# Constant 16-bit matmuls placed in TensorE's waits inside each norm of a ten-stage transformer kernel

## What is computed

```python
def rmsnorm(x, g):
    xf = x.astype(jnp.float32)
    y = xf * lax.rsqrt(jnp.mean(xf * xf, axis=-1, keepdims=True) + RMS_EPS)
    return (y * g.astype(jnp.float32)).astype(x.dtype)

def first_block(x, ...):
    for l in range(DEPTH):
        x = x + 0.5 * _swiglu(_rms_norm(x, ffn1_norm[l]), ffn1_w_gu[l], ffn1_w_down[l])
        x = x + _hybrid_mixer(_rms_norm(x, mix_norm[l]), w_in[l], ...)
        x = x + 0.5 * _swiglu(_rms_norm(x, ffn2_norm[l]), ffn2_w_gu[l], ffn2_w_down[l])
    return _rms_norm(x, final_norm)
```

## Time and profile before

| | us |
|---|---|
| median of three runs | 1652.29 |
| the profiled execution, its own time | 1651.31 |
| its span, from the first to the last instruction | 1649.5 |
| TensorE matmuls busy (97% of the span) | 1594.4 |
| GpSimd busy | 1000.3 |
| VectorE busy | 504.5 |
| ScalarE busy | 366.6 |
| mean granted TensorE clock | 0.976 of full speed |

### The profile page before, as it was taken

The page is one execution under the profiler, slowest core; times in us unless marked ns, Lnnn a source line. Parts: engine busy times, 40 slices in busy tenths (PEclk is TensorE's granted clock), DMA queues, the critical chain, the costliest instruction groups (busy, mean ns, idle before and its releaser), DMA issues.

```text
span 1649.5 us, 32224 instructions
## 1 busy us (share of the span) xinstructions
PE 1594.4 (97%) x14172; PEld 1396.0 (85%) x14172; DVE 504.5 (31%) x1128; ACT 366.6 (22%) x902; POOL 1000.3 (61%) x542
## 2 busy tenths in 40 slices
PE   7999999999999999999999999979999999999998
PEld 5888788887888888878888888868788887788887
DVE  3111264343110211125534311133433233533323
ACT  2111124212110211111422211023333122324212
POOL 6777555666777577764566677744165664346571
PEclk9999999999999999999999999979989999989999
DMA  9565444554555465544455555534354554434461
GB/s 358 202 205 205 141 173 160 179 205 163 200 203 203 176 214 201 201 167 154 162 176 201 178 201 198 197 104 158 132 175 144 198 179 164 150 127 167 173 205 52
DMA packets 42619, 294.90 MB, mean 179 GB/s; under 512 B 4720, under 2 KB 6256, under 8 KB 7792
## 3 DMA queue, kind: packets, MB, share of 16 engines
q1 hardware_dynamic: 42480, 292.84, 50.9%
HBM read 291.78 MB, written 1.05 MB: 178 GB/s over the span
## 4 chain that ended last, share of the span: by engine, by line
PE 95%; DVE 2%; ACT 1%; issue 1%; POOL 0%; DMA 0%; SPq 0%; DVEq 0%; ACTq 0%
PE ps L510 27%; PE ps L511 27%; PE ps L512 27%; PE ps L528 2%; PE ps L530 1%; PE ps L529 1%; PE ps L760 1%; PE ps L596 1%; PE ps L602 1%; PE ps L614 1%; PE ps L588 1%; PE ps L586 0%; DVE diag L1199 0%; POOL w_low L486 0%; DMA ring<-in_w 0%
## 5 line engine op out<-in xcount | busy, mean ns | idle before, releaser
L486 POOL TENSOR_TENSOR w_low<-ring 128x1024 f16<-128x1024 f32 (+2 forms) x538 | 1000.1, 1883 | 616.6 <-DMA ring<-in_w 616.5
L510 PE MATMUL ps<-hP,ring 128*128 128x256 f16 (+1 forms) x2976 | 820.5, 276 | 14.1 <-DVE hP L1209 11.7
L511 PE MATMUL ps<-hP,ring 128*128 128x256 f16 (+1 forms) x2976 | 819.9, 276 | 0.0
L512 PE MATMUL ps<-hP,w_low 128*128 128x256 f16 (+1 forms) x2976 | 819.3, 275 | 0.0
L510 PEld LDWEIGHTS ps<-hP,ring 128*128 128x128 bf16 (+1 forms) x2976 | 294.7, 99 | 62.3 <-DVE hP L1209 13.8
L511 PEld LDWEIGHTS ps<-hP,ring 128*128 128x128 bf16 (+1 forms) x2976 | 294.7, 99 | 36.9
L512 PEld LDWEIGHTS ps<-hP,w_low 128*128 128x128 f16 (+1 forms) x2976 | 294.9, 99 | 36.6
L511 PE MATMUL ps<-work,ring 128*128 128x256 f16 x1088 | 296.7, 273 | 0.0
L510 PE MATMUL ps<-work,ring 128*128 128x256 f16 x1088 | 296.5, 272 | 0.0
L512 PE MATMUL ps<-work,w_low 128*128 128x256 f16 x1088 | 296.3, 272 | 0.0
L1242 DVE TENSOR_TENSOR ps<-work,ps 128x256 f32<-128x256 f32 x88 | 37.8, 429 | 342.1 <-PE ps L512 312.0
(11 more groups left out here) (199 smaller groups left out, 1142.2 us busy)
## 6 DMA issues: line engine op xcount, KB each, us to landing
ring<-in_w SPq DMA_DIRECT2D x268, 1024.0 KB, 4.8
con<-in_const SPq DMA_DIRECT2D x1, 2732.0 KB, 16.6
gm<-in_gm SPq DMA_DIRECT2D x2, 1024.0 KB, 16.9
ring<-in_w SPq DMA_DIRECT2D x2, 640.0 KB, 5.9
ring<-in_w SPq DMA_DIRECT2D x2, 560.0 KB, 3.9
ring<-in_w SPq DMA_DIRECT2D x2, 544.0 KB, 3.7
xT<-in_x SPq DMA_DIRECT2D x4, 256.0 KB, 3.8
out<-work SPq DMA_DIRECT2D x8, 128.0 KB, 2.0
```

Of the source, the lines that this page charges most:

```text
L486: nc.gpsimd.tensor_tensor(w_low[:, c % SLOTS, a:b], ring[:, c % SLOTS, a:b], w_high[:, c % SLOTS, a:b], ALU.subtract).then_inc(split.by((c ...
L510: nc.tensor.matmul(bank, w_high[:, slot, a:a + m], rhs(k, 0), start=(k == 0), stop=False)
L511: nc.tensor.matmul(bank, w_high[:, slot, a:a + m], rhs(k, 1), start=False, stop=False)
L512: mm = nc.tensor.matmul(bank, w_low[:, slot, a:a + m], rhs(k, 0), start=False, stop=(k == kt - 1))
```

## The change

TensorE's program gets a helper, `idle_work(n)`, which issues n matmuls of a 128 by 128 stationary and 256 moving columns, both taken from `ones` and read as 16-bit numbers, into bank 3. In every norm 5 stand between the two sums (L546 and L549), and 8 between the second sum and the first spreading product (L549 and L552). In the eight inner norms 14 more stand behind the second spreading product (L554), ahead of the stage's first tile. B0 has 40 more at its very start, ahead of its first wait. No wait and no signal is added, removed or moved.

```diff
+                def idle_work(n):
+
+                    for _ in range(n):
+                        nc.tensor.matmul(ps[:, 3, 0:T], ones[:, 0:HD].bitcast(BF16), ones[:, :].bitcast(BF16), start=True, stop=True)
+
                 def norm(s):
+                    if s == "B0":
+                        idle_work(40)
                     pe.wait_ge(*summed.at((s, DK - 2)))
                     for t in range(TT):
                         nc.tensor.matmul(ps[:, 1 + t, 0:1], acc[:, t * P:t * P + P], ones[:, 0:1], start=True, stop=False)
+                    idle_work(5)
                     pe.wait_ge(*squared.at((s, DK - 1)))
                     for t in range(TT):
                         mm = nc.tensor.matmul(ps[:, 1 + t, 0:1], sq[:, 1, t * P:t * P + P], ones[:, 0:1], start=False, stop=True)
                     mm.then_inc(stat_done.by(s), 1)
+                    idle_work(8)
                     pe.wait_ge(*diag_a.at(s))
                     nc.tensor.matmul(ps[:, 7, 0:P], ones[:, :], diag[:, 0:P], start=True, stop=True)
                     pe.wait_ge(*diag_v.at(s))
                     nc.tensor.matmul(ps[:, 7, P:T], ones[:, :], diag[:, P:T], start=True, stop=True
                                      ).then_inc(spread.by(s), 1)
+                    if s in inner:
+                        idle_work(14)
```

## The result

The changed kernel takes 1633.96 us at the median of four executions, against 1652.45 for the kernel before, measured beside it; the ratio is 0.9885, with a 95% interval of 0.9871 to 0.9899. A second measurement (e9) gave 0.9878 (0.9862 to 0.9895). The forecast was 1636.5, the range 1633 to 1645. The profiled execution took 1634.92 us, with a span of 1633.1 and a mean granted clock of 0.993.

The account below looks back on a forecast made before the run. TensorE was taken as the bound, slowed by a low clock behind norms. Savings of 13.3, 2.1 and 0.5 us, less 0.5 for hand-overs, gave 15.4 off 1651.3; with the median 1.0 higher, 1636.9, stated as 1636.5, range 1633 to 1645.

Parts of the forecast that it names:

- seven stretches: Dense matmuls behind seven norms, 27.30 us at clock 0.50; full clock there was to save 13.3 us.
- Rival 1: The clock falls although TensorE multiplies constants, and the added matmuls run slowly: 1665 us, chance 0.06.
- rival 4: The clock already holds in reality and something else slows those 27 us: 1652 us, chance 0.01.
- gaps of the norms behind F0, float32 products and hand-overs: Spreading products and sums at the low clock in the norms: 2.1 us saved, less 0.5 for hand-overs.
- F0: First norm, at the kernel's start: between 0.8 us lost and 1.3 gained, taken as 0.5 us gained.
- 0.6 for B0: B0's norm: sums save 0.7 and spreading products 0.4, but the five stand in the way for 0.55.
- F2's 0.4: F2's norm: both spreading products leave the low clock, saving 0.4 us.
- The hand-overs: Possible delay where added matmuls give way to the norm's own work: 0.5 us, between 0 and 2.
- terms of 1.07, 0.6 and 0.9: F0's delays at the low clock: five cost 1.07 us, eight 0.6, fourteen take 3.0 where 2.1 are there.
- less 1.03: In F0 the first tiles lose 1.03 us anyway, waiting for GpSimd's low part until 17.85.
- Rival 2: The clock holds in the short norms and falls in B0, despite the forty: 1641 us, chance 0.12.
- Rival 3: The clock falls in about half of the norms, the work being too thin: 1645 to 1650 us, chance 0.05.

Follow-up runs that it names:

- e9: The changed kernel measured once more, unaltered: 1632.66 us, ratio 0.9878 to the kernel before.
- e3: The changed kernel with the same 282 added matmuls at 16 moving columns each in place of 256: 1653.89 us, ratio 0.9997.
- e2: The changed kernel without the fourteen; the five, the eight and B0's forty stay: 1639.05 us, ratio 0.9898.
- e5: The changed kernel with twenty-eight added matmuls in place of the fourteen: 1643.60 us, ratio 0.9944.
- e1: The changed kernel without the five and the eight; the fourteen and B0's forty stay: 1642.40 us, ratio 0.9921.
- e6: The changed kernel with no added matmuls in F0: 1635.82 us, ratio 0.9896.
- e8: The changed kernel, with L760's 15-column float32 products in B0 and B1 also interleaved among dense matmuls: 1626.64 us, ratio 0.9840.
- e10: e8 without the five in F0 and B0, with 28 added ahead of F0's first wait and fifty for B0's forty: 1629.02 us, ratio 0.9858.

## Why the prediction was right, point by point

**The bound and the mechanism.** Shown, and forecast so. What slowed the seven stretches was TensorE's clock; it fell in the gaps because too little was streamed in them (e3: the same instructions, narrow, and nothing changes), and constants do keep it up. Rival 1 falls with the seven rows at 1.00, rival 4 with them. Whether other data would do as well as ones wasn't tried.

**The size of it.** The profiled pair of executions (span 1649.5 and 1633.1) splits the 16.4 us by the starts of the stages:

| term | forecast | found |
|---|---|---|
| seven dense stretches | 13.3 | 13.3, the sum of what each first tile's distance to the next norm lost |
| gaps of the norms behind F0, float32 products and hand-overs | 2.1 - 0.5 = 1.6 | 1.7 |
| F0 | 0.5 | 1.2 |
| N2 and the end | in the 2.1 | 0.2 |
| sum | 15.4 | 16.4 |

The gaps, from the last dense matmul to the first tile, were 5.85, 5.72, 5.51, 5.98, 5.50, 15.52 and 5.86 us in A0, F1, F2, A1, F3, N1 with B0, and B1; they are 5.75, 5.53, 5.54, 5.61, 5.60, 14.42 and 5.75. The largest single term outside the dense stretches is B0's, 1.10, for which the forecast had 0.9 (0.3 for N1 and 0.6 for B0). F2's 0.4 didn't come, because TensorE wasn't all that its gap hung on. VectorE's half of the diagonal took 0.75 us before and 1.16 after, so that the second product had to wait and stands 0.76 us behind the first, not 0.58. First F2's two rows, before and after, then B1's in the changed kernel and in e9, its repetition:

```profile
553.50 0.75 DVE L1199 TENSOR_SCALAR diag<-con,rcol 128x128 f32<-128x128 f32 x1
548.19 1.16 DVE L1210 TENSOR_SCALAR diag<-con,rcol 128x128 f32<-128x128 f32 x1
1356.53 1.37 DVE L1210 TENSOR_SCALAR diag<-con,rcol 128x128 f32<-128x128 f32 x1
1357.52 0.29 DVE L1210 TENSOR_SCALAR diag<-con,rcol 128x128 f32<-128x128 f32 x1
```

This one instruction takes 0.29 us (in N2, where GpSimd is idle) to 1.95 us (in A1 of e2), and moves single gaps by up to 0.75 us (B1: 5.75 in the changed kernel, 5.00 in e9). In e9 the same gaps gained 2.8 us over the kernel before. So that 1.6 met 1.7 is in part luck; the 13.3 isn't. The prediction had no term for this instruction.

**The hand-overs.** Taken at 0.5 between 0 and 2; they are about 0 at the high clock (F1's distances above; 1.94 or 1.95 us to the first tile with and without the fourteen). The cover was sized right: e5 shows that it ends with the fourteenth.

**F0** is the term that was mis-sized, 0.5 against 1.2 (1.7 in e9, with the same code). Its timeline after the change, which answers to the earlier trace rows:

```profile
9.83 0.85 PE L557 MATMUL ps<-ones,sq 128*128 128x1 f32 x4
...
13.49 2.62 PE L546 MATMUL ps<-ones 128*128 128x256 bf16 x14
15.94 0.27 PE L510 MATMUL ps<-hP,ring 128*128 128x256 f16 x1
...
18.37 0.28 PE L510 MATMUL ps<-hP,ring 128*128 128x256 f16 x1 [1.28 <-POOL w_low L486]
```

L557 comes 0.87 us later (1.1 said), but the first tile only 1.32 (14.62 to 15.94), half of what the forecast's terms of 1.07, 0.6 and 0.9 add up to, since the clock rose under the fourteen. And the next low part from GpSimd releases TensorE at 18.37, only 0.52 behind the 17.85 of before; and the clock was up from 15.37, not from 21.4. The 3.55 us that TensorE had run densely at the low clock (17.85 to 21.4), by 0.488, are 1.73; less 0.52 that leaves 1.2. The forecast had let the clock rise 1 to 4 us earlier; it was 6. Its delay was mis-added as well: those three terms less 1.03 give 1.5 and not 0.8, while 0.52 was measured.

**B0.** L553 waits 1.12 us for VectorE's sums (1.3 said), behind the forty:

```profile
1083.79 4.53 PE L546 MATMUL ps<-ones 128*128 128x256 bf16 x40
1089.43 0.61 PE L553 MATMUL ps<-ones,acc 128*128 128x1 f32 x4 [1.12 <-DVE acc L1203]
```

Rival 2 didn't come about in either profile of the changed kernel; how near it lay no run shows. Rival 3 did not either; e1 and e2 are what it looks like, with half the filler: the clock falls in some norms and holds in others, for the same instructions. Its forecast of 1645 to 1650 was too high for it: the execution of e1 that lost four norms took 1638.0 us and the slowest 1643.6, since the dense stretches lose little where the clock rises again under the fourteen.

**The signs that were named.** Tiles 0.109 us apart behind each norm: yes. The mean clock was said to go to 0.985 and went to 0.993; this was careless, since 27.3 us at half speed are 0.008 of the span alone, and the gaps and N1's stretches came on top. Two signs misled. "If the first tile has no wait, the fourteen are too many": the row has no wait, and e2 shows that they cost nothing; the hole that is left is just too small to be shown. L552's wait for ScalarE's diagonal was to stay, and is down to this (total, times, longest), without anything having become later:

```profile
PE ps L553 <- DVE acc L1203: 9.1, 2, 8.0
...
PE ps L561 <- ACT diag L937: 0.2, 1, 0.2
```

Of the signs of being wrong none came: every norm behind F0's begins earlier, and although single diagonals took longer, VectorE's and ScalarE's halves of the diagonal take 10.9 and 4.0 us in all ten norms, against 10.6 and 4.0 before. The sign that works is the distance between two starts on the critical path, before and after.

**From the execution to the median.** The profiled pair differs by 16.4 us and the medians (1652.45 and 1633.0) by 19.4: the profiled execution of before lay 1.1 us below its median, that of after 1.9 above. The forecast of 1636.5 was thus 3.5 us too high: 1.0 is missing in the sum, and most of the rest comes from which executions happened to be profiled, which the forecast couldn't know. That executions of one kernel differ by 1 to 3 us has at least three sources in the profiles. Between the changed kernel's and e9's (1.4 us) F0 makes 0.5 and the gaps with VectorE's diagonal 1.0. L760's low stretches are a third: they come to 20.48 us in these two (6.83 and 13.65, and 10.24 twice), but to 17.07 in e5 and e6 (10.24 and 6.83), which is worth 1.7 us. It is why e6's profile (1632.8) is no longer than the changed kernel's (1633.1), although F0 costs it 1.0.

## What to carry to other kernels

Where TensorE is the bound and a clock row dips behind short gaps, wide 16-bit matmuls on constants in the waits keep the clock, and what they bring can be forecast from the windows of before: half of each dense stretch that reads 0.50. Size each group to the wait that covers it, by the distance between starts on the critical path, fill the gap from its first wait on, and stop short of its end, since each matmul beyond is paid in full, and at double price if the clock is already low. Where narrow matmuls pull the clock down themselves, no filler is needed: put them between dense ones.

## What the runs showed of the hardware

- TensorE's clock follows what is streamed, not whether TensorE is busy. The 15-column float32 matmuls read busy for 10.24 of 10.24 us at a clock of 0.50; 282 added matmuls of 16 columns left every low stretch in place (0.9997), and 282 of 256 columns removed those of the norms (0.9885).
- A gap need not be one long wait. In F1's of before no wait was longer than 1.46 us, and the clock fell.
- With a filling that is just too thin, whether the clock falls is a matter of the single gap: with the same instructions in each norm, four of eight lost it in e1's profile and three of eight in e2's.
- VectorE's instructions slow down beside GpSimd's: 0.36 to 1.29 us and 0.56 to 2.23 us for the same two (e8 and e10). VectorE's half of a norm's diagonal takes between 0.29 and 1.95 us for the same work, and single gaps differ by it from execution to execution (B1: 5.75 and 5.00 us). An earlier start elsewhere can bring this about (argued from e8 and e10, one profile of each).
